# Half of a stage's gate products moved behind the attention products, and two attention outputs put into one PSUM bank

## The reference, cut to what matters

```python
s = einsum('bqhmd,bkhmd->bhmqk', qi, k) * scale + bias
pr = softmax(s)
a = pr[:, :, 0] - lam * pr[:, :, 1]
o = einsum('bhqk,bkhe->bqhe', a, v)
att = rmsnorm(o, g_subln) * (1 - lam_init)
...
gates = sigmoid(u @ w_gate + b_gate)          # 1024 x 2048 weights
merged = g_a * (att @ w_att_up) + g_s * (ssm @ w_ssm_up)
```

## Time and profile before

| | us |
|---|---|
| median of 3 runs | 3187.9 (3187.07 to 3191.05) |
| profiled execution | 3191.59 |
| its span, first to last instruction | 3190.1 |
| `attend`, first issue to last copy of its output | 771.65 to 1086.6 |
| `turn_attention`, first issue to last copy of a gate | 1334.33 to 1507.7 |

### The profile page before, as it was taken

One profiled execution on the slowest core, in us unless ns is written; L12 is line 12 of the kernel. 1 busy time (PEld: TensorE's weight loads), 2 busy tenths in 40 slices (PEclk: granted clock), 3 DMA queues, 4 the chain that ended last, 5 costly groups with the idle time before them and its releaser, 6 DMA issues. The chain is left out here.

```text
span 3190.1 us, 41940 instructions
## 1 busy us (share of the span) xinstructions
PE 2760.1 (87%) x15536; PEld 2364.5 (74%) x15536; DVE 1641.2 (51%) x2216; ACT 1309.3 (41%) x1848; POOL 284.7 (9%) x323
## 2 busy tenths in 40 slices
PE   3999999796667679688797796589999999999798
PEld 2789888585555447577586685589999999999687
DVE  5100000261788687540564225767777777777555
ACT  4111111151566664431443212245555555555445
POOL 1000000000000100020111001101011010110112
PEclk6999999898798799889799897589999999999899
DMA  8422211274230234473974764178788787887442
GB/s 280 104 81 67 99 66 61 80 240 132 80 88 11 69 112 130 142 237 116 310 250 155 226 197 167 55 229 252 239 247 259 242 248 236 247 259 239 137 174 93
DMA packets 451003, 530.92 MB, mean 166 GB/s; under 512 B 18680, under 2 KB 387208, under 8 KB 449896
## 3 DMA queue, kind: packets, MB, share of 16 engines
q1 hardware_dynamic: 421232, 412.91, 41.4%
q0 software_dynamic: 29664, 116.57, 11.6%
HBM read 401.30 MB, written 128.12 MB: 166 GB/s over the span
## 5 line engine op out<-in xcount | busy, mean ns | idle before, releaser
L2128 DVE TENSOR_TENSOR ex_w_lo<-ex_w_raw,ex_w_hi 128x2048 fp32r<-128x2048 f32 x195 | 443.9, 2291 | 143.0 <-ACT ex_w_hi L2085 143.0
L2217 PE MATMUL ex_ps_u<-ex_x,ex_w_hi 128*128 128x384 f32 x2048 | 411.7, 341 | 5.1 <-DVE ex_w_lo L2128 5.1
L2085 ACT ACTIVATE ex_w_hi<-ex_w_raw 128x2048 fp32r<-128x2048 f32 x195 | 370.4, 1908 | 0.8
L2217 PEld LDWEIGHTS ex_ps_u<-ex_x,ex_w_hi 128*128 128x128 f32 x2048 | 349.1, 189 | 6.1 <-issue 5.5
L2217 PEld LDWEIGHTS ex_ps_u<-ex_x,ex_w_lo 128*128 128x128 f32 x2048 | 266.2, 192 | 0.6
L2217 PE MATMUL ex_ps_u<-ex_x,ex_w_lo 128*128 128x192 f32 x2048 | 266.0, 273 | 0.0
L2236 PE MATMUL ex_ps_d<-ex_w_hi,ex_h 128*128 128x512 f32 x768 | 265.8, 400 | 0.0
L354 DVE TENSOR_TENSOR w_lo<-w_raw,w_hi 128x2048 fp32r<-128x2048 f32 x15 | 34.3, 2289 | 404.4 <-ACT w_hi L322 404.4
L328 ACT ACTIVATE stage<-ps 128x512 f32<-128x512 f32 (+1 forms) x102 | 55.8, 547 | 415.0 <-PE ps L376 359.6
L2236 PE MATMUL ex_ps_d<-ex_w_lo,ex_h 128*128 128x512 f32 x512 | 202.9, 396 | 0.0
L2236 PEld LDWEIGHTS ex_ps_d<-ex_w_hi,ex_h 128*128 128x128 f32 x768 | 144.6, 188 | 35.0
(11 more groups left out here) (385 smaller groups left out, 5221.7 us busy)
## 6 DMA issues: line engine op xcount, KB each, us to landing
ex_w_raw<-in_w_exp_gate SPq DMA_DIRECT2D x64, 1024.0 KB, 5.2
ex_w_raw<-in_w_exp_up SPq DMA_DIRECT2D x64, 1024.0 KB, 6.1
ex_w_raw<-in_w_exp_down SPq DMA_DIRECT2D x64, 1024.0 KB, 6.7
w_raw<-in_w_in SPq DMA_DIRECT2D x15, 1024.0 KB, 5.5
mg_w_raw<-in_w_ssm_up SPq DMA_DIRECT2D x24, 512.0 KB, 5.4
mg_g_raw<-g_d SPq DMA_DIRECT2D x24, 512.0 KB, 7.3
xbcT_d<-stage POOLq DMA_DIRECT2D x5, 1536.0 KB, 5.6
cv_raw<-xbcT_d POOLq DMA_DIRECT2D x10, 768.0 KB, 5.7
```

The source lines that it names most:

```text
L2085: act.activation(w_hi[:, j % CUT], w_raw[:, j % RAW], ACT.Copy).then_inc(w_hi_done, 1)
L2128: dve.tensor_tensor(w_lo[:, j % CUT], w_raw[:, j % RAW], w_hi[:, j % CUT].bitcast(F32), ALU.subtract).then_inc(w_split, 1)
L2217: last = pe.matmul(ps_u[:, j % 2, m, 0:wide * C], w[:, s, k, cols], x[:, k, 0:wide].rearrange("p a c -> p (a c)"), start=i == 0, stop=i == ...
```

## The change

- `turn_attention` makes its 8 gate tiles only for tokens 768 to 1535: two chunks of 384 tokens (`CHUNK`, `chunks=(2, 3)`) in place of three blocks of 512. That is 16 units of 24 products with 384 columns.
- `attend` makes the same 8 gate tiles for tokens 0 to 767 (`chunks=(0, 1)`): 16 "fills" of 24 products with 384 columns. They stand in slices of up to 12 (long step) or 8 (short step) behind the products with v in each step, from step 2 to step 40, and none in the three steps between the chunks, when POOL loads the other half of `u`. So a fill is two long steps or three short ones.
- The fill's weights come by POOL's queue. ACT splits their high part (line 812) and copies a finished gate tile (line 818); POOL makes the low part (line 778). All are single buffers: `w_raw`, `w_hi`, `w_lo`, `gst`, `ps_g`.
- The first slice of a fill waits for `w_hi` of that fill, which ACT makes behind both exponentials of the same step. The products with `w_lo`, last in a fill, wait for POOL.
- To make room in PSUM for `ps_g`, the attention's two output tiles share one bank, and PE waits for the copies of unit k-4 before it writes unit k-3; ACT therefore makes these copies first in its step. The mixed map `a` has one buffer, and DVE waits until the one before is turned. The outputs are stored in groups of 4 tiles.
- The gates lie in memory as [2, 8, 128, 1536] rather than in blocks of 512 tokens. The pieces that are read and written there stay rows of 512 tokens, or of 384 from the two stages.

```diff
-def attend(nc, qkT_d, v_d, line_d, lam_params, ident, o_d):
+def attend(nc, qkT_d, v_d, line_d, lam_params, ident, o_d, u_hi_d, u_lo_d, w_gate, gate_tiles, chunks, g_d):
...
+    GROUPS = 4
+    FIRST_FILL, REST, QUOTA = 2, 3, {T1: 12, T2: 8}
...
-        ps_o = ctx.enter_context(nc.psum_tensor("at_ps_o", [P, 2, BLK], F32))
+        ps_o = ctx.enter_context(nc.psum_tensor("at_ps_o", [P, 2, 2 * P], F32))
+        ps_g = ctx.enter_context(nc.psum_tensor("at_ps_g", [P, BLK], F32))
...
+            load_w(0)
+            load_u(0)
+            split_lo(0)
+            load_w(1)
             for j, (head, g0, b, L) in enumerate(UNITS):
...
+                for f in range(NF):
+                    if ends[f] + 1 == j + LATE or (j == 0 and ends[f] + 1 < LATE):
+                        store_gate(f)
+                        if (f + 1) % NTL == 0 and f + 1 < NF:
+                            load_u((f + 1) // NTL)
+                        if f + 1 < NF:
+                            split_lo(f + 1)
+                        if f + 2 < NF:
+                            load_w(f + 2)
...
+                for f in range(NF):
+                    if ends[f] + 1 == k:
+                        copy_gate(f)
+                        if f + 1 < NF:
+                            split_hi(f + 1)
                 if 2 <= k < NU + 2:
...
-                    if j >= 2:
-                        dve.wait_ge(turned, j - 1)
+                    if j:
+                        dve.wait_ge(turned, j)
...
-                    if j >= 2:
-                        pe.wait_ge(o_copied, j - 1)
+                    if j:
+                        pe.wait_ge(o_copied, j)
...
+                if k in slices:
+                    for n in range(*slices[k]):
+                        f, i = n // WHOLE, n % WHOLE
+                        if i == 0:
+                            pe.wait_ge(w_hi_done, f + 1)
+                            pe.wait_ge(u_in, 32 * (f // NTL + 1))
+                            if f:
+                                pe.wait_ge(g_copied, f)
+                        if i == 2 * KT:
+                            pe.wait_ge(w_split, f + 1)
+                        w, u = ((w_hi, u_hi), (w_hi, u_lo), (w_lo, u_hi))[i // KT]
+                        last = pe.matmul(ps_g[:, 0:CHUNK], w[:, i % KT], u[:, i % KT], start=i == 0, stop=i == WHOLE - 1)
```

More of the change, by code:

```diff
@@ L26 @@
 BLK = 512
+CHUNK = 384
 NB = T // BLK
@@ L683, in attend @@
     STEPS = NU + LATE
+    GROUPS = 4
+    FIRST_FILL, REST, QUOTA = 2, 3, {T1: 12, T2: 8}
+    NTL = len(gate_tiles)
+    FILL = [(col, n) for n in chunks for col in gate_tiles]
+    NF, WHOLE = len(FILL), 3 * KT
+    slices, done = {}, 0
+    for k in range(FIRST_FILL, NU + 3):
+        f = done // WHOLE
+        if f < NF and not (f == NTL and done % WHOLE == 0 and k < max(m for m in slices if slices[m][1] == NTL * WHOLE) + REST):
+            n = min(QUOTA[UNITS[min(k, NU - 1)][3]], WHOLE - done % WHOLE)
+            slices[k] = (done, done + n)
+            done += n
+    assert done == NF * WHOLE
+    ends = {(b // WHOLE) - 1: k for k, (a, b) in slices.items() if b % WHOLE == 0}
+    w_view = w_gate.rearrange("(k p) c -> p k c", p=P)
     v_in = v_d.rearrange("(i p) c -> p i c", p=P)
@@ L763, in _ @@
                     act.activation(v[:, hs, :, 0], v_raw[:], ACT.Copy).then_inc(hi_split, 1)
+                if k >= LATE:
+                    j = k - LATE
+                    head, g0, b, L = UNITS[j]
+                    act.wait_ge(pv_full, j + 1)
+                    if j % 4 == 0 and j >= 4 * GROUPS:
+                        act.wait_ge(o_stored[j // 4 % GROUPS], 16 * (j // 4 // GROUPS))
+                    if j >= 2:
+                        act.wait_ge(o_added, j - 1)
+                    whole = inv[:, j % (LATE + 2), 0:1]
+                    act.activation(o[:, j // 4 % GROUPS, j % 4], ps_o[:, j % 2, 0:P], ACT.Copy, scale=whole)
+                    act.activation(beside[:, j % 2], ps_o[:, j % 2, P:2 * P], ACT.Copy, scale=whole).then_inc(o_copied, 1)
+                if k == 1:
+                    split_hi(0)
                 if k < NU:
@@ L1271, in _, with turn_attention @@
             sum_squares(NC - 1)
-def turn_attention(nc, o_rows, gain_row, ident, hi_d, lo_d, u_hi_d, u_lo_d, w_gate, gate_tiles, g_d):
+def turn_attention(nc, o_rows, gain_row, ident, hi_d, lo_d, u_hi_d, u_lo_d, w_gate, gate_tiles, chunks, g_d):
     G, RING, AHEAD = VD, 4, 2
@@ L1279, in turn_attention @@
     NTL = len(gate_tiles)
-    UNITS = [(i, col, blk) for blk in range(NB) for i, col in enumerate(gate_tiles)]
+    UNITS = [(i, col, n) for n in range(len(chunks)) for i, col in enumerate(gate_tiles)]
     NG = len(UNITS)
@@ L1421, in _ @@
                         pe.wait_ge(u_lo_in[blk], 16)
-                    last = pe.matmul(ps_g[:, s], w[:, i, k], u[:, k, toks], start=j == 0, stop=j == len(terms) - 1)
+                    last = pe.matmul(ps_g[:, s, 0:CHUNK], w[:, i, k], u[:, k, toks], start=j == 0, stop=j == len(terms) - 1)
                 last.then_inc(g_full, 1)
```

100 lines of the change are left out of this document (62 added, 38 removed).

## The result

The changed kernel takes 3208.2 us (median of 4 runs, 3206.7 to 3209.4), the kernel before 3189.1 beside it: a ratio of 1.006, 95% interval 1.0042 to 1.0077. It is **slower by 0.6%**, inside the range of the prediction and on the side that it forecast, 9 us above its time. The profiled execution took 3209.43 us, its span is 3207.9 us, against 3190.1 before: +17.8.

What follows compares the result with a forecast made beforehand. PE was taken to bound `turn_attention`, a DVE and ACT ring `attend`'s long steps. 3191.6 + 66 (`attend`) + 7 (its start) - 62 (`turn_attention`) = 3202.6 us profiled, median 3199, +0.35%; range 3182 to 3214.

Steps and rivals of the forecast that it cites:

- a ring through DVE and ACT: `attend`, long steps before the change: low part, first map's bias and minimum, two exponentials, high part set 5.73 us per step.
- The stage that loses products: `turn_attention`: fewer, narrower gate products shorten it from 150.2 to 87.8 us, -62 us, bounds -67 to -58.
- the stop: `turn_attention`: PE's wait for the fifth weight tile, queued behind a load of `u`, goes from 9.75 to 8.2 us.
- Long steps: `attend`: PE waits 2.2 us for `w_hi`; two steps grow from 11.46 to 15.4 us, 43 us over 11 fills.
- Short steps and the reload: `attend`: five fills in short steps cost +2.2 us each, 11 us; waiting for the other half of `u`, 4 us.
- The clock: `attend`: PE's new waits drop the clock to 1.2 GHz, 1.7 us each, 5 or 6 of 14 times: 10 us.
- The steps of the heads' splits: `attend`: two fills begin in steps where PE stands still for a head's split anyway: -2 us.
- The start: Start of `attend`: POOL's 3.67 MB of weights and `u` share the transfer engines with the first head's data: +7 us.
- Edits at nothing: `attend`'s shared bank, single `a` buffer and POOL's queued addition, and the gates' new layout: no cost.
- POOL beside DVE: `attend`: POOL's low part starts after DVE's mixing is over, so their shared port costs 0; a lagging POOL is a rival.
- The second: Rival in `attend`: `w_hi` is ready before PE needs it; -29 us, 3159 us; chance 0.07.
- The first: Rival: clock and start of `attend` cost nothing; -5 us, 3183 to 3194 us; chance 0.24.

Runs made afterwards that it cites:

- the spare work: Changed kernel plus 16 spare transposes behind the products with v in every step where a fill after the first begins: 3200.3 us, ratio 1.0027.
- the last two runs: Split ahead of exponentials, later first loads, slices of 8: slice ahead of turning in three split steps, 3142.9 us; then also 24 spare transposes, 3140.8 us.
- the cures of each alone: Changed kernel with 16 spare transposes per later fill's start, 3200.3 us; changed kernel with POOL's first loads waiting for the first head's data, 3197.4 us.
- the run with the other edits alone: Kernel before plus only `attend`'s edits without gate work (shared bank, copies first, one `a` buffer, stores of four tiles): 3187.4 us, ratio 0.9992.

## Why the prediction was right

**What bounds the stages.** Right. `turn_attention` loses what its products take, `attend` turns from a ring through DVE and ACT into a row of PE's own work, and the wait for `w_hi` stands on it: 12 waits of 2.2 us on average, where about 14 of 2.2 were forecast.

**The stage that loses products.** -60.9 for -62. Inside it the stop was mis-sized: 11.13 us, not 8.2, and above the 9.75 it was before. By the earlier trace rows PE was through with its four units 1392.31 - 9.75 - 1356.85 = 25.71 us after the first product; now it is 1468.04 - 11.13 - 1435.55 = 21.36. So PE came 4.35 us earlier, where 2 were put, although the prediction's own prices give 4 x 24 x (0.227 - 0.179) = 4.6. The weights let it go on 32.49 us after the first product for 35.46, 2.97 earlier, where 3.5 were put: 9.75 + 4.35 - 2.97 = 11.13. The "some 20 us" to the tile's landing don't come out of the earlier trace rows either, where its split starts 34.35 us after the first product. The rest was 89.3 - 68.7 - 11.1 = 9.5 us, where 9.9 and 1 for a longer chain were put: that chain cost nothing that can be seen. (576 products of 0.227 us are 130.8, not 130.6; nothing hangs on it.)

**Long steps.** 8.8 and 6.56 us were forecast; with the clock held they were 9.11 and 6.55. The estimate from the ring's rows, 5.04 us from the first map to `w_hi`, is 4.97 in the trace. But not every fill pays this. Over the same steps before, from mixing to mixing, the eleven fills in two long steps cost 44.6 us, of which 11.4 are the clock in six of them: 33 us, where 43 were put and 2 taken off for the splits. The first of the eleven costs 0.2 us, the last 2.4.

**Short steps and the reload.** The other five fills cost 2.3, 5.6, 6.6, 3.7 and 3.7 us, 21.9 in all, of which 4.5 are the clock in three of them: 17.4 us, where 11 were put, and 4 for the reload of `u`, which made PE wait 2.7 in the third.

**The clock.** The mechanism was right, the size too small: 10 us were put for 5 or 6 falls at 1.7. (The lower bound of 54 for `attend`, "clock holds", is also 2 below the prediction's own sum without the clock, 56.) In the changed kernel nine steps are longer than the same steps with the spare work (six long, two short, and the reload of `u`), seven by about 1.5 us and two by 2.5 and 2.8: about 16 us. From first to last mixing the kernel with spare work is only 10.2 us shorter, since the spare work makes others longer, 5.3 us in the three steps behind the splits.

**The steps of the heads' splits.** Forecast -2, because PE stands still there anyway; the two in which a fill begins became 0.9 and 2.4 us longer with the step behind them. PE does stand still, but it comes out of it at 1.2 GHz, and its first products behind it are on the path: in the last two runs the clock held with 24 spare transposes there (1.00 for 0.50), and the step went from 8.6 to 6.2 us. That is the one step whose sign was wrong. Together all steps gave +69 for +66.

**The start.** +7 was taken from even sharing, with 13.5 as the bound if all of POOL's 3.67 MB came first at 271 GB/s. It was +10.5. All of POOL's data had landed, by 792.6, when the last of the head's came in for the split at 795.69, and 3.67 MB at the 354 GB/s of that stretch are 10.4 us. The failing choice is the even sharing. POOL's data did not simply go first, though: by the GB/s of its 2 us stretches some 6.2 MB had moved from 775 to 793, so 2.5 of them were SP's. The rate of the bound was too low, since the 271 GB/s are a mean over the head's data and the slower bias behind them.

**Edits at nothing.** Right, 0.9992 of the kernel before when those of `attend` stand alone. The layout of the gates had no run of its own; all that lies outside the two sums below is 17.8 - 18.7 = -0.9 us.

**POOL beside DVE.** Right for the changed kernel: DVE's mixings are 1.28 us as before. The meeting came only when the split was moved, and at another instruction than the mixing. There the rows show DVE's low part of v at 3.89 us while POOL's 3.25 us run. The Trainium skill, SBUF — State Buffer, section SBUF: two separate sides, says that whichever of a GpSimd instruction and a DVE instruction with two SBUF inputs starts first has the shared port pair until it ends. The trace agrees step by step: POOL's addition waits for DVE's low part of q (1.50 us for 0.45), DVE's next one for the addition (2.01 for 1.75), POOL's low part for that one (3.25 for 2.38), and the low part of v for POOL's; and beside it DVE's instruction with one input from PSUM keeps its 1.22 us.

**The rivals.** The second, PE not meeting the wait, was priced at 3159; made by reordering ACT it came to 3166.8. Of the 7.8 us between them the start is 3.5, and the two meetings of POOL and DVE are 4.3 in the trace. That this is the whole of it is not shown: the price also left out the clock, which that kernel does not hold either (0.88 behind its second split). The first, without clock and start, was wrong since both were there: the cures of each alone gave back 8.0 and 10.9 us. If these add up, which no run tried, they lead from 3208.2 to 3189.3, where that rival stood.

**Sum.** +79.6 - 60.9 = 18.7, against 73 - 62 = 11 forecast. The 7.7 between them are the start (3.5), the steps (69.1 for 66) and `turn_attention` (1.1). Inside the steps the errors cancel: the long fills came to 33 for 41, the short ones with the reload to 17.4 for 15, the clock to 16 for 10. That 69 is so close to 66 is partly luck.

## What to carry to other kernels

When work is put into an engine's idle time, look not only at how much idle time there is but at where in the step its operands become ready: here an operand split behind two long instructions on another engine cost more than the products did, and moving it 5 us earlier in the step, into that engine's own pause, turned a loss of 0.6% into a gain of 0.75%. An idle stretch of TensorE can cost twice where the work behind it is on the path: here nine of the 13 waits before gate products were followed by 1.4 to 2.8 us lost at the lower clock. Spare work in the pause can be cheaper than none, as long as it doesn't outlast the pause. Loads for later that are issued in the same moment as the loads for now can land ahead of them, so let them wait for the data that are wanted now.

## What the runs showed of the hardware that was not expected

- 16 spare transposes in a pause of about 2.2 us kept TensorE at 2.4 GHz behind it: the granted clock was 1.00 from 1050 to 1120, for 0.95 and 0.90 without them. 24 of them behind a slice of gate products, in PE's wait of some 9 us for a head's split, did too (1.00 for 0.50).
- POOL's queue was given 3.67 MB within 2 us of the first loads on SP's. All of POOL's had landed by 792.6, the first head's data on SP's queue only by 795.7, 10.5 us later than without them. The two queues together moved 354 GB/s over 15 us.
- A POOL addition of 128 columns takes 1.50 us in place of 0.45 when it starts beside a DVE low part with two inputs from SBUF. It does so at three splits also in the run with the other edits alone, which has no gate work in `attend`.
